# A decoder block with gathered experts: tiles of 4 slots of 32 tokens instead of 2 of 64, products on four column quarters, and a chunk streamed in two halves

## The reference

```
h  = rmsnorm(x);  proj = h @ w_in
y  = [retention(4 heads), gated_delta_rule(4 heads)]   # chunks of 128 tokens, a state passed on
x  = x + y @ w_out
h2 = rmsnorm(x);  q = h2 @ wq                          # 8 heads, 2 halves of 128
s1, s2 = q_half . sub_keys (128 each);  top 16 of each -> 256 sums -> top 16
ids = i1 * 128 + i2;  gate = softmax(best)
x  = x + sum over 128 slots (gate * gelu(u_tab[ids] . h2)) * v_tab[ids]
out = rmsnorm(x) * lnf_w
```

## Time and profile before

| | |
|---|---|
| median of 3 runs | 3082.02 us (3080.98 to 3084.36) |
| profiled execution, its own time | 3079.45 us |
| its span, first to last instruction | 3077.5 us |
| PE busy | 2353.2 us (76%) |
| VectorE busy | 2084.6 us (68%) |
| ScalarE busy | 1181.0 us (38%) |
| GpSimd busy | 1162.0 us (38%) |
| moved by DMA | 1265.79 MB, mean 411 GB/s |
| mean granted clock of PE | 0.89 |

### The profile page before, as it was taken

The page is one execution under the profiler, slowest core; times in us unless marked ns, Lnnn a source line. Parts: engine busy times, 40 slices in busy tenths (PEclk is TensorE's granted clock), DMA queues, the critical chain, the costliest instruction groups (busy, mean ns, idle before and its releaser), DMA issues.

```text
span 3077.5 us, 36445 instructions
## 1 busy us (share of the span) xinstructions
PE 2353.2 (76%) x12400; PEld 1352.1 (44%) x12400; DVE 2084.6 (68%) x5601; ACT 1181.0 (38%) x3458; POOL 1162.0 (38%) x1030
## 2 busy tenths in 40 slices
PE   8876787987875787996885678797787577865555
PEld 7753355753441354762562245564355124511111
DVE  4476856669579855658649974666856986496454
ACT  2243444334434444235323542434443443233222
POOL 0132442334333432333434444333443444354443
PEclk9998899998997899998997899899898789987777
DMA  8399999999999999999999999999999999999998
GB/s 350 145 407 426 417 427 425 425 427 419 426 426 420 416 417 425 403 426 426 424 425 427 413 426 424 424 425 426 413 426 421 425 415 422 427 418 420 427 427 340
DMA packets 178890, 1265.79 MB, mean 411 GB/s; under 512 B 21648, under 2 KB 21904, under 8 KB 26256
## 3 DMA queue, kind: packets, MB, share of 16 engines
q0 software_dynamic: 147456, 1073.81, 83.3%
q1 hardware_dynamic: 28368, 183.72, 14.4%
q10 hardware_dynamic: 2880, 5.94, 0.5%
HBM read 1259.19 MB, written 4.19 MB: 411 GB/s over the span
## 4 chain that ended last, share of the span: by engine, by line
PE 35%; DMA 30%; DVE 22%; ACT 8%; issue 4%; POOL 1%; ACTq 0%; POOLq 0%; DVEq 0%
DMA uv<-uv_tab,ids 23%; PE bank L580 12%; DVE uv L1417 10%; PE bank L641 9%; DMA wbuf<-w 7%; PE bank L633 7%; PE bank L648 2%; DVE area L1500 2%; ACT diag L1033 2%; POOL uv L545 1%; ACT actT L1068 1%; DVE area L1745 1%; PE bank L663 1%; DVE area L1741 1%; PE bank L608 1%
## 5 line engine op out<-in xcount | busy, mean ns | idle before, releaser
L545 POOL DMA_INDIRECT uv<-uv_tab,ids x1024 | 1161.5, 1134 | 1888.2 <-PE bank L580 1555.9
L1417 DVE CUSTOM_DVE_ANT_0 uv<-uv,h 128x1024 f32<-128x1024 f32 x1024 | 1237.3, 1223 | 733.1 <-DMA uv<-uv_tab,ids 726.3
L580 PE MATMUL bank<-uv,diag 128*64 128x512 f32 x4096 | 1167.1, 701 | 519.1 <-ACT diag L1033 518.3
L580 PEld LDWEIGHTS bank<-uv,diag 128*64 128x64 f32 x4096 | 283.2, 153 | 1172.2 <-ACT diag L1033 743.7
L1027 ACT ACTIVATE gelu<-dots 128x2 f32<-128x2 f32 x512 | 104.2, 204 | 1467.2 <-DVE dots L1417 1466.8
L641 PE MATMUL bank<-actT,wbuf 128*128 128x128 f32 x2688 | 337.7, 287 | 39.4 <-DMA wbuf<-w 32.6
L641 PEld LDWEIGHTS bank<-actT,wbuf 128*128 128x128 f32 x2688 | 324.7, 201 | 86.6 <-issue 67.9
L1033 ACT ACTIVATE diag<-gated,gelu 128x64 f32<-128x64 f32 x1024 | 300.7, 340 | 60.5 <-ACT gelu L1027 2.8
L1023 ACT ACTIVATE gated<-smalls,gate 128x64 f32<-128x64 f32 x1024 | 294.2, 336 | 8.2 <-DVE acc L1428 8.2
L633 PE MATMUL bank<-wbuf,actT 128*128 128x256 f32 x960 | 227.1, 390 | 27.5 <-DMA wbuf<-w 22.4
L633 PEld LDWEIGHTS bank<-wbuf,actT 128*128 128x128 f32 x960 | 180.5, 193 | 98.7 <-issue 49.7
(11 more groups left out here) (235 smaller groups left out, 1886.1 us busy)
## 6 DMA issues: line engine op xcount, KB each, us to landing
wbuf<-w SPq DMA_DIRECT2D x146, 1024.0 KB, 9.2
uv<-w SPq DMA_DIRECT2D x20, 1024.0 KB, 18.8
uv<-uv_tab,ids POOLq DMA_INDIRECT x1024, 16.0
acc<-x SPq DMA_DIRECT2D x8, 512.0 KB, 13.8
y<-acc ACTq DMA_DIRECT2D x14, 256.0 KB, 9.0
rowbuf<-x SPq DMA_DIRECT2D x5, 512.0 KB, 12.4
actT_ahead<-x SPq DMA_DIRECT2D x3, 512.0 KB, 18.6
keys_sb<-keysT ACTq DMA_DIRECT2D x1, 1024.0 KB, 14.1
```

Source lines behind the costliest of these rows:

```text
L545: nc.gpsimd.indirect_dma_start(out=uv[i % RING][:, :, :].rearrange("p z d -> p (z d)"), out_offset=None, in_=uv_tab, in_offset=bass.Indire ...
L580: done = mm(sums[s // PAIRS][z][64 * j:64 * j + 64, :], diag[:, i % DIAGS, :], uv[i % RING][:, 1, 512 * z:512 * z + 512], start=False, sto ...
L1417: V.tensor_tensor_reduce(out=u, in0=u, in1=h2[n % 2][:, j, :], scale=1.0, scalar=0.0, op0=ALU.mult, op1=ALU.add, accum_out=dots[:, i % DOT ...
```

## The change

A tile holds four slots of 32 tokens. Partitions 32q to 32q+31 hold slot q of a quad. A step takes two tiles j = 0, 1, which are the tokens 64h+32j to 64h+32j+31 of half h. A chunk has 64 turns still, but the first 32 work off all 128 slots of its first 64 tokens, the other 32 those of the second 64.

- *Products.* `diag` has 32 columns; the four products of a step write to the four quarters of 32 partitions of one PSUM bank: quarter 64j + 32z for tile j and channel half z. A bank holds one half of the tokens.
- *Ids and gates.* Written in 16 blocks of 32 partitions instead of four of 64. All eight heads of a chunk are now needed within its first 32 turns.
- *h2.* PE makes rows of the normed tokens (`normed_rows`, two banks, copied to `hrows` with the scaling), and eight times per chunk `spread` makes from them a bank in the order of the tiles (four products with 32 output rows), which ScalarE copies to `h2` (`spread_out`). The eight are done at set turns (`SPREAD`): four for the first half at turns 54 to 60 of the chunk before, four for the second half at turns 2 to 8.
- *Norm per half.* After each half one square, an exchange of the two channel halves' sums by four small copies, a root, one scaling and four stores of 32 rows.
- *Schedule.* `STAGES` has other ends. `ropes` has one buffer instead of two, and the loads of `acc` wait for `x2_taken` alone.

```diff
-PAIRS = SLOTS // 2
-STEPS = NCH * PAIRS
+QUADS = SLOTS // 4
+TURNS = 2 * QUADS
+STEPS = NCH * TURNS
-FINISH = 3
-SUMS_FREE = 6
+FINISH, ROOT, STORE, SUMS_FREE = 3, 5, 8, 8
+SPREAD = {54: (1, 0, 0), 56: (1, 0, 1), 58: (1, 0, 2), 60: (1, 0, 3), 2: (0, 1, 0), 4: (0, 1, 1), 6: (0, 1, 2), 8: (0, 1, 3)}
-STAGES = [("route", -1, -1), ("mix", 0, -3), ("route", 0, 22), ("mix", 1, 52), ("route", 1, 86), ("mix", 2, 117),
-          ("route", 2, 139), ("mix", 3, 172), ("route", 3, 208), ("mix", 4, 242), ("route", 4, 264), ("mix", 5, 300),
-          ("route", 5, 336), ("mix", 6, 371), ("route", 6, 393), ("mix", 7, 432), ("route", 7, 454)]
+STAGES = [("route", -1, -1), ("mix", 0, -3), ("route", 0, 13), ("mix", 1, 43), ("route", 1, 76), ("mix", 2, 106),
+          ("route", 2, 130), ("mix", 3, 162), ("route", 3, 198), ("mix", 4, 232), ("route", 4, 256), ("mix", 5, 292),
+          ("route", 5, 328), ("mix", 6, 363), ("route", 6, 387), ("mix", 7, 424), ("route", 7, 448)]
...
+                for j in range(2):
+                    for z in range(2):
+                        i, o = 2 * s + j, 64 * j + 32 * z
+                        made = mm(sums[n][half][o:o + 32, :], diag[:, i % DIAGS, :], uv[i % RING][:, 1, 512 * z:512 * z + 512],
+                                  start=False, stop=(quad == QUADS - 1), skip_group_check=True)
+                made.then_inc(v_used, 1)
...
+            def spread(n, part, i):
+                j, z = divmod(i, 2)
...
+                pe.wait_ge(*event("hrows", n, part))
+                of, t0 = slice(64 * z, 64 * z + 64), 64 * z + 32 * j
+                for q in range(4):
+                    made = mm(free[32 * q:32 * q + 32, :], ident[of, t0:t0 + 32], hrows[of, part, :], start=True, stop=True)
+                made.then_inc(spread_made, 1)
...
+            def spread_out(n, part, i):
...
+                A(h2[part][:, j, 512 * z:512 * z + 512], bank_of[n, f"rep{4 * part + i}"][:, :], ACT.Copy).then_inc(S["rep"], 1)
+            def finish(n, part):
...
+                A(y_half[:, :], sums[n][part][:, :], ACT.Square, scale=D ** -0.5, accum_out=st[:, 58:59]).then_inc(S["yss"], 1)
...
-                    here = slice(TOPK // 2 * a, TOPK // 2 * z)
-                    quarters = [(q, j, slice(64 * q, 64 * q + 64), slice(64 * j, 64 * j + 64)) for q in range(2) for j in range(2)]
+                    here = slice(TOPK // 4 * a, TOPK // 4 * z)
+                    blocks = [(q, j, slice(32 * q, 32 * q + 32), slice(32 * j, 32 * j + 32)) for q in range(4) for j in range(4)]
...
-                    for q, j, into, of in quarters:
+                    for q, j, into, of in blocks:
                         last = V.tensor_tensor(
...
```

More of the change, by code:

```diff
@@ L115, in uses_of @@
     outs, h2T = own(("out0", "x2", 2, 0), ("out1", "x2", 2, 1)), own(("h2T0", "h2T", 2, both), ("h2T1", "h2T", 2, 1))
-    rep = own(*[(f"rep{i}", "rep", 4, i) for i in range(4)])
+    rep = own(*[(f"rows{i}", "hrows", 2, i) for i in range(2)])
     if kind == "start":
@@ L976, in rest_of_queries @@
                 scores_of(0, "s0b", (2, 3))
-                replicate(0)
+                normed_rows(0)
+                for i in range(4):
+                    spread(0, 0, i)
                 for j, f in ((1, 0.2), (2, 0.3), (3, 0.35)):
@@ L1431, in _, with finish @@
-            upto = Stream(peer_turn, 2, lambda step: step >= STEPS or step < chosen_pairs[0])
+                if QUADS < step < STEPS and quad in (FINISH + 1, ROOT + 1) and j == 1:
+                    (finish if quad == FINISH + 1 else scale)(*divmod(2 * n + half - 1, 2))
+            def finish(n, part):
+                dve.wait_ge(*event("yss", n, part))
+                for j in range(2):
+                    for z in range(2):
+                        here, there = 64 * j + 32 * z, 64 * j + 32 * (1 - z)
+                        last = V.tensor_copy(st[here:here + 32, 59:60], st[there:there + 32, 58:59])
+                last.then_inc(peer_chain, 1)
+                dve.wait_ge(peer_chain, 2 * (2 * n + part) + 1)
+                V.tensor_tensor(st[:, 59:60], st[:, 58:59], st[:, 59:60], ALU.add).then_inc(S["y_sum"], 1)
```

260 lines of the change are left out of this document (145 added, 115 removed).

## The result

| | before | after |
|---|---|---|
| median | 3081.5 us (3080.5 to 3084.4, 4 runs) | 3163.5 us (3162.5 to 3165.4, 4 runs) |
| ratio | | 1.0265, 95% interval 1.0247 to 1.0283 |
| span of the profiled execution | 3077.5 us | 3162.5 us |
| VectorE busy | 2084.6 us | 2195.0 us |
| PE busy, its granted clock | 2353.2 us, 0.890 | 2119.5 us, 0.764 |

The direction of the prediction was right and its size was not: +82 us where +14.5 stood, and 3163.5 lies far outside 3073 to 3121.

What follows compares the result with a forecast made beforehand. It took DMA transfers at 427 GB/s as the bound. Lag 18, products -2, spread 0, start 0, norm -1.5 gave +14.5 us: 3094 for the profiled execution, 3096.5 for the median; own range 3088 to 3108, with rivals 3073 to 3121.

Steps and rivals of the forecast that it cites:

- The question is who eats the 10 us of queue: Before the DMA engines: about 10 us of queued gathers, so a late engine costs nothing until it has eaten them.
- the weight-loading stretches still at 426: Sign to check: transfers in stretches that load weights would stay at 426 GB/s after the change.
- VectorE's instructions: Ids and gates in 16 + 16 instructions: 0.172 us each, 4.1 us more a group, 103 us of VectorE over 25 groups.
- The low bound of 0.08 us: Ids and gates: instructions starting 0.08 us apart would add only 1.2 us a group; called unlikely.
- rival B: Faster: small VectorE instructions overlap and quarters give back what PE held; middle, start and end win, 3072 us; chance 0.14.
- What they cost: Routings without weight streams and what follows: VectorE's lag outlasts the queue, +18 us, bounds 0 and 40.
- Rival C: Much slower: each 4.1 us lump falls on an empty queue and chunk 0's squeezed routing starves the ring; +40 us, 3120; chance 0.13.
- Start: First gathers and chunk 0's routing, squeezed from 25 to 16 steps: it fits, 0 us, bounds -5 and +8.
- Quarters: Value products four side by side: a step takes some 1.1 or 1.9 us; 2 us back at 1240 to 1280, bounds 0 and 4.3.
- rival D: Value products on quarters don't run side by side: 3.4 us a step at full clock, 3200 us and more; chance 0.03.
- Spread: Rows, then spread: eight spreads a chunk on PE and ScalarE, which have room; 0 us, bounds 0 and 5.
- Tail: End of the kernel, per-half norm: shorter last products, one square and one scaling fewer, five small VectorE instructions; -1.5 us, bounds -3 and +1.

Runs made afterwards that it cites:

- e1: Changed kernel with its gather buffers moved to begin at a multiple of 512 bytes, by allocating the same tensors in another order: 3132.4 us, ratio 1.0172.
- e5: Changed kernel with gather buffers at a multiple of 512 bytes and 4 + 4 instead of 16 + 16 id and gate instructions (partly wrong values): 3096.3 us.
- e4: Kernel before with ids and gates written by 16 + 16 instructions of 32 partitions, same result: 3119.1 us, ratio 1.0126.
- e9: Kernel before with the changed kernel's STAGES alone, the routing of chunk 0 ending at turn 13 instead of 22: 3099.9 us, ratio 1.0058.
- e12: Changed kernel with buffers at a multiple of 512 bytes, 4 + 4 id and gate instructions (partly wrong values), second-half spreads at turns 20 to 26: 3089.4 us.
- e6: Changed kernel with gather buffers at a multiple of 512 bytes and second-half spreads at turns 20 to 26 instead of 2 to 8: 3123.3 us, ratio 1.0132.

## Why the prediction failed, step by step

*The bytes' rate.* "The question is who eats the 10 us of queue" took 427 GB/s as given, and the check named "the weight-loading stretches still at 426". This is the step that failed first: it has no term in the sum. It is not alone: with the address undone e1 still stands at 3132.4, outside 3073 to 3121, because the terms for the instructions, the start and the spreads were too small (below). The diff did bear on it, since it resizes tensors ahead of the gather buffers, but nothing in the one trace of before shows a second address. Measured 31 to 38 us. I had bounded idle time and not the rate.

*VectorE's instructions.* 0.172 us each and +103 us of VectorE: measured 0.168 and 0.163, +97.1 us (132.2 - 35.1). Right, though not "whatever their width": the earlier trace rows has 8 columns in both, and at 32 columns the four take 0.86 and 0.79 us. The low bound of 0.08 us is refuted, and rival B with it.

*What they cost.* The term was 18 us with bounds 0 and 40, for these instructions and the shorter stages together. Measured for the instructions alone: 36 us between e1 and e5, 38 us in e4. The mechanism was right: 5.3, 8.6 and 9.0 us at the starts of mixes 3, 5 and 7 (e1 less e5 in the table) and 3.9 behind chunk 7, where the sum had 4, 4, 4 and 3. The rest lies in stretches for which the sum had 3 in all, 4.7 us of it from 300 to 880. The size was off, as I read the timeline, because the lag was spread evenly over 19 steps. The work comes in a piece of 6.5 us, and at the end of the routing it meets the mixing's 5 us piece with one dot product between. The sum of durations over the steps can't show that; the timeline at the hand-over in the trace of before could have (2.2 us and then the convolution, with GpSimd standing 9.35 us already). Rival C named this lump and the starved start, at +40 us, and got 0.13; with the address undone the kernel is at +51, and of all cases C is the nearest.

*Start.* 0, bounds -5 and +8, "it fits". Measured +15: the sum over the whole stretch fits (VectorE has half its time free from 200 to 280 in e9), its first 40 us don't, and the 80 us behind them lose as much again. The first gather was put at 137 and came at 134.77: its ids take 2.71 us instead of 0.69, but begin at 131.77 where they began at 133.93; what made them begin earlier was not looked into, and 2 us are of no weight here.

*Quarters.* 1.06 and 1.94 us where 1.1 and 1.9 stood. Right, and rival D is refuted. The 2 us back at 1240 to 1280 are seen in the table (1060 to 1640 loses 3.5 instead of 7.4), but e9 without the quarters has 1.8 there, so the stages may have done it. What the quarters by themselves give was not run. The page "TensorEngine Tiling (Array Packing)" of the Trainium skill, section "Theoretical Speedup", has up to 4x for a dimension of 32; against one such product after another no run here measures it, against the halves it is 1.94/1.06 = 1.83. What it brought with it was a lower clock (0.764), and at that low clock e12 is 7 us above the kernel before, which bounds what it cost.

*Spread.* 0, bounds 0 and 5, with the remark that "four of them at the start of a mixing stage" sit in the in-order streams. Measured 7 to 9 us (e6, e12): the remark named the place, and it had no price. By which wait they cost this is open.

*Tail.* -1.5 us. In e1 the last products start at 3119.33, 8.9 us ahead of the end of the span; before, 9.3 (3068.24 of 3077.5). One scaling of 0.75 and one square fell away as said.

```profile
3119.33 1.93 PE L581 MATMUL bank<-uv,diag 128*32 128x512 f32 x8 [2.95 <-ACT diag L1071]
...
3122.05 0.62 DVE L1489 COPY st<-st 32x1 f32<-32x1 f32 x4 [3.66 <-ACT y_half L1096]
...
3124.64 1.76 ACTq L1109 DMA_DIRECT2D y<-y_half  x4
```
But the four small copies take 0.62 us, four stores take 1.76 us of issue instead of 1.00, and the products are no shorter at the low clock (1.93 against 1.94). -0.4, inside the bounds.

*The sum as measured*, by undoing one after the other: address 31, instructions 36, spreads 7, rest 7 (the stages among it, 17.6 when alone in the kernel before), 81 in all of 82. The rest is small because some stretches lose less than before (11.0 us against 20.9 in e12), while the start loses 12 more.

## What to carry to other kernels

Where a kernel lives on its DMA rate, a diff that resizes or reorders any tensor in SBUF ahead of the transfer buffers changes something that no instruction shows: compare the GB/s of the undisturbed slices first, and place those buffers explicitly (here at a multiple of 256 bytes). A queue of 10 us was no cover for 4.1 us more in a group's end. By the timeline it is each unbroken piece of work on the engine that lets the buffers go that has to be set against the queue, the two pieces on both sides of a stage boundary together. And that the work of a squeezed stage fits its length says too little: here it fitted, and 15 to 18 us were lost, about half of them at its head.
